# A split of the weight ring, a later clearing of a scratch table, and three changes of order in a two-block transformer kernel

## The chip, the cores and the metric

The kernel runs on one core of a Trainium2 chip. The metric is the device time of one execution in microseconds (us), the median of several runs; lower is better. Engines are named as the profile names them: PE is TensorE, which multiplies matrices (PEld is its weight load), DVE is VectorE, ACT is ScalarE, POOL is GpSimd and SP is SyncE, which issues most of the DMAs.

## What is computed

Two transformer blocks in float32 for one sequence of 256 tokens and a width of 2048. Cut to its stages:

```python
# first block
n1 = rms_norm(x, norm1_gain);  proj = n1 @ w_in          # latents, k_pe, q/k/v of the window heads
o_mla = 8 heads of latent attention (w_q_b, w_kv_b, rope, causal softmax)
o_swa = 16 heads of attention in a window of 128, bias from a table, sinks
h = x + concat(rms_norm(o_mla), rms_norm(o_swa)) @ w_out
q = rms_norm(h) @ peer_w_q;  s = q . sub_keys            # 8 heads, top 16 of 16384 experts for each
y = sum over the chosen experts of  g * gelu(h . expert_u) * expert_v;   h = h + y
# second block
qa, ka, va, qn, kn, vn, gates = rms_norm(h) @ w_in_2
oa = differential attention of 4 heads;   on = neighbourhood attention of 8 heads with a bias
mixed = sigmoid(g_a) * (oa @ w_branch_a) + sigmoid(g_b) * (on @ w_branch_b)
x = h + rms_norm(mixed @ w_out_2)
u = relu(rms_norm(x) @ w_up) ** 2;   out = x + rms_norm(u @ w_down)
```

## The kernel before

All weights stream through one ring. They are cut into 1101 pieces of 128 x 1024 float32 (512 KB), in the fixed order of the list `order`. SP loads a piece into one of five slots of `raw` (L2748). PE multiplies in a reduced float format, so each piece is split in two: ACT writes the rounded high part into one of NH = 3 slots of `whi` (L1872), and DVE then writes the rest, `raw - whi`, into one of three slots of `wlo` (L2102). The activations are split in the same manner: `AA` and `BB` hold 16 blocks of 128 rows with a high half (`AH`, `BH`) and a low half (`AL`, `BL`). A product is then high x high + low x high + high x low. `gemm_piece` keeps the activations as weights in PE and moves the piece past them: 8 matmuls with `whi` and then 4 with `wlo`. `wide_piece` (the stages `peer_w_q`, `peer_u` and `w_up`) keeps the piece in PE and moves the activations past it: 8 matmuls of 512 columns with `whi`, then 8 of 256 columns with `wlo`.

The semaphores of the ring: `hi_split` counts the pieces that ACT split, `lo_split` those that DVE split, and `piece_used` those that PE has finished with. ACT waits for the landing of piece n and for `piece_used` of piece n - 3, DVE waits for `hi_split` of n, SP waits for `lo_split` of n - 5 before it loads n.

The order of work on every engine is written by one function, `walk`. It runs once for each engine; all five runs go through the same steps, and each engine emits only its own instructions. `piece` and `used_up` call `ensure_split`, which puts the loads and splits of the next pieces into the order. Smaller work (transposes, softmax, evacuations) stands in generators in `tasks` and `idle`; `step()` advances each by one `yield` between two pieces. Each engine works strictly in the order that comes out. `fresh(engine, tokens)` leaves out waits that the engine has already passed, and `latest["PE"]` is the last PE mark emitted so far in the walk.

Places that the change and the prediction touch:
- The expert gates are kept in a DRAM table `scr_g` of 16384 x 256 values (16.8 MB). POOL blanks a tile of 128 x 256 (`gate_blank`, L2688) and issues eight DMAs of 2 MB that write zeros from it (`gate_clear`, L2694). Much later POOL adds the chosen gates with 256 indirect DMAs (`gate_scatter`, L2699). In the walk `gate_blank` stands after `queries(1)` of the latent attention; before the change it waits for nothing.
- `k_rope` builds zero-padded rotary keys in two rounds, both in the one slot of `prows`. Each round has a `zero` on POOL (a memset of 128 x 1024, L2680), then `spread_kpe` on DVE (in the trace under L2355), transposes on PE (L1723) and splits. In the order of POOL the first `zero` stands ahead of `gate_blank` and the second one directly behind the eighth `gate_clear`. The scores of the latent attention (`mla_scores`) wait for the splits of both rounds.
- POOL's next instruction after that is `reload_x` (L2685).
- `attend` is the softmax pipeline of all attention units. Behind the exponentials (ACT, L1914) there is one `yield`, then PE turns the probabilities (L1723). `na_unit` uses it for a head of the neighbourhood attention, two units at a time, between the pieces of `w_in_2`.
- `prepare(sc)` multiplies the fetched gelu values by the fetched gates (`expert_gate`, DVE L2507) and splits them into `AA` (ACT L1857, `expert_split` DVE L2514), in four rounds with a `yield` behind each. The first gemm of `peer_v` needs the result of `prepare(0)`. Before, `prepare(0)` is put into `idle` when u is 61, so it runs between the pieces of the units 62 and 63 of `peer_u`. After each unit `u_post` runs: ACT L1857 copies the low sums, DVE L2492 adds, DVE L2498 scales, ACT applies gelu.

Of the kernel before, what the change touches and what calls it, by code (L numbers as in the profile page):

```python
# [37 lines left out]
def build(nc, D, out):  # L38
# [12 lines left out]
    with ExitStack() as ctx:  # L51
# [144 lines left out]
        s_hi, s_lo, s_used = sem("hi_split"), sem("lo_split"), sem("piece_used")  # L196
        s_vec = sem("vector_step")

        def walk(steps):
# [189 lines left out]
            def gemm_wide(name, units, both, toks, post, lead=2):  # L389
                taken = [take(accs) for _ in units]  # L390
                for c in range(4):
                    while len(toks) < min(2 * c + lead, 8):
                        step(0)
                    for n, (u, (pair, free)) in enumerate(zip(units, taken)):
                        i, low = piece(name, 4 * u + c)
                        high = fresh("PE", (s_hi, i + 1))
                        b = [banks[2 * pair], banks[2 * pair + 1]]
                        go("mm_wide", i, b, c, both, high, low, fresh("PE", toks[2 * c:2 * c + 2], free))
                        last = used_up()
                        if c == 3:  # L400
# [105 lines left out]
            def attend(scores, U, nk, scale, sink, pslots, blocks, pv, finish, combine=None, per_head=None, added=None):  # L506
# [30 lines left out]
                yield  # L537
# [388 lines left out]
            go("gate_blank")  # L926
# [422 lines left out]
            def na_unit(h):  # L1349
# [297 lines left out]
        def tensor_program(e):  # L1647
# [7 lines left out]
            def gemm_piece(i, b, c, n, lh, ll, high, low, free, kks=(0, 1)):  # L1655
# [5 lines left out]
                for kk in kks:  # L1661
                    kt = 2 * c + kk
                    w = slice(512 * kk, 512 * kk + 512)
                    for t in range(2):
                        a = slice(128 * t, 128 * t + 128)
                        mm(b[t][:, :], lh[:, kt, a], whi[:, s, w], kt == 0, False)
                        mm(b[t][:, :], ll[:, kt, a], whi[:, s, w], False, False)
# [11 lines left out]
            def gemm_rows(held, t, b, n, lh, ll, free):  # L1679
# [3 lines left out]
                for i, c, split in held:  # L1683
# [3 lines left out]
                    for kk in range(2):  # L1687
# [3 lines left out]
                        mm(b[t][:, :], lh[:, kt, a], wlo[:, s, w], False, False)  # L1691
                        last = mm(b[t][:, :], ll[:, kt, a], whi[:, s, w], False, kt == 2 * n - 1)
                    if t == 1:
                        last.then_inc(s_used, 1)
# [3 lines left out]
            def wide_piece(i, b, c, both, high, low, free):  # L1698
                s = i % NH
                for mark in free:  # L1700
                    e.wait_ge(*mark)
                for mark in high:
                    e.wait_ge(*mark)
                for kk in range(4):
                    kt = 4 * c + kk
                    x = both[:, kt, :, :].rearrange("p a n -> p (a n)")
                    for m in range(2):
                        w = slice(256 * kk + 128 * m, 256 * kk + 128 * m + 128)
                        mm(b[m][:, :], whi[:, s, w], x, kt == 0, False)
                for mark in low:  # L1710
                    e.wait_ge(*mark)
                for kk in range(4):
                    kt = 4 * c + kk
                    for m in range(2):
                        w = slice(256 * kk + 128 * m, 256 * kk + 128 * m + 128)
                        last = mm(b[m][:, 0:256], wlo[:, s, w], both[:, kt, 0, :], False, kt == 15)
                last.then_inc(s_used, 1)
# [15 lines left out]
            def kpe_mm(i, bank, split, free):  # L1733
# [6 lines left out]
                for kt in range(16):  # L1740
                    w = slice(64 * kt, 64 * kt + 64)
                    mm(o, whi[:, s, w], AH[:, kt, :], kt == 0, False)
                    mm(o, wlo[:, s, w], AH[:, kt, :], False, False)
                    last = mm(o, whi[:, s, w], AL[:, kt, :], False, kt == 15)
# [56 lines left out]
            def sub_scores(i, c, q4, t, bank, end, split, ready):  # L1801
# [5 lines left out]
                for m in range(4):  # L1807
# [5 lines left out]
                    mm(o, AH[:, hp, a], wlo[:, s, w], False, False)  # L1813
                    last = mm(o, AL[:, hp, a], whi[:, s, w], False, True)
# [35 lines left out]
            walk({"consts": consts, "mm": gemm_piece, "mm_rows": gemm_rows, "mm_wide": wide_piece, "transpose": transpose, "bias_mm": bias_mm,  # L1850
# [4 lines left out]
        def scalar_program(e):  # L1855
# [205 lines left out]
        def vector_program(e):  # L2061
# [604 lines left out]
        def gpsimd_program(e):  # L2666
# [20 lines left out]
            def gate_blank():  # L2687
                e.memset(blank, 0.0).then_inc(sem("gate_blank"), 1)  # L2688
# [206 lines left out]
```

## Time and profile before

| | us |
|---|---|
| median of 3 runs | 3259.15 |
| range of the runs | 3258.58 to 3262.24 |
| the profiled execution | 3259.14 |
| its span, first to last instruction | 3257.3 |
| PE busy in it | 3200.2 (98%) |
| DVE busy | 2106.2 (65%) |
| ACT busy | 1517.7 (47%) |
| mean granted clock of TensorE | 0.994 |

The profile is of one execution. Its time is the span and 1.8 us around it. A row of the timeline gives the start in us from the span's start, the duration in us, engine, line, operation, out<-in, shapes and how many instructions were merged, and in square brackets how long the engine was idle before it and what released it. "POOL", "DVE" and so on are the engines; an SPq row is the issue of a DMA. The profile's clock is the share of full speed that TensorE was granted: 1.00 is 2.4 GHz and 0.50 is 1.2 GHz.

### The profile page before, as it was taken

The numbers are of one execution on the slowest core, as the hardware profiler recorded it, in microseconds if no ns is written. First come the engines' busy times: TensorE is split into PE (matmuls) and PEld (weight loads), VectorE is DVE, ScalarE is ACT, GpSimd is POOL, SyncE is SP. The second block draws the span as 40 slices with busy tenths as digits, with TensorE's granted clock in tenths as the row PEclk, the third lists the DMA queues.
The fourth block names the chain that finished last, engine by engine and source line by source line (L and its number), as shares of the span: only waits on it lengthen the run. The fifth ranks groups of instructions, "written<-read, shape, count | busy, mean of one in ns | idle before, by whom it ended". The sixth has DMA issues, their size and how long they took to land.

```text
span 3257.3 us, 40800 instructions
## 1 busy us (share of the span) xinstructions
PE 3200.2 (98%) x16112; PEld 2715.7 (83%) x16112; DVE 2106.2 (65%) x3062; ACT 1517.7 (47%) x2006; POOL 492.0 (15%) x322
## 2 busy tenths in 40 slices
PE   8989999999999999999999999999999999999998
PEld 7788888888888888888888888888888788888886
DVE  6766578887555576666666565565465655655556
ACT  5645454545444444444444544445444544444443
POOL 1000005777777200000000000000000000000000
PEclk9999999999999999999999999999999999999999
DMA  8623557888888866666665555444555455555554
GB/s 321 252 85 130 181 183 208 214 214 215 212 214 211 262 249 244 250 248 245 245 233 200 197 184 174 165 170 176 191 194 188 174 192 191 193 189 193 189 192 149
DMA packets 220286, 660.95 MB, mean 203 GB/s; under 512 B 56704, under 2 KB 56848, under 8 KB 217536
## 3 DMA queue, kind: packets, MB, share of 16 engines
q1 hardware_dynamic: 170864, 600.81, 52.9%
q0 software_dynamic: 49232, 57.54, 8.7%
q8 instruction: 127, 2.08, 0.3%
q14 instruction: 63, 0.52, 0.0%
HBM read 622.48 MB, written 35.78 MB: 202 GB/s over the span
## 4 chain that ended last, share of the span: by engine, by line
PE 90%; DVE 6%; ACT 2%; issue 1%; DMA 1%; DVEq 0%; ACTq 0%; SPq 0%
PE PS L1649 89%; DVE wlo L2102 2%; PE PS L1723 2%; ACT whi L1872 1%; DMA raw<-in_w_in_b 0%; DVE R L2606 0%; ACT M L1914 0%; DVE AA L2148 0%; ACT Y L1958 0%; DVE TMP L2177 0%; DVE M L2507 0%; DVE TMP L2178 0%; DVE BB L2148 0%; DMA R<-in_x 0%; DMA M<-in_na_bias 0%
## 5 line engine op out<-in xcount | busy, mean ns | idle before, releaser
L2102 DVE TENSOR_TENSOR wlo<-raw,whi 128x1024 fp32r<-128x1024 f32 x1101 | 1343.8, 1224 | 889.6 <-ACT whi L1872 878.4
L1872 ACT ACTIVATE whi<-raw 128x1024 fp32r<-128x1024 f32 x1101 | 1157.8, 1057 | 1033.4 <-PE PS L1649 998.3
L1649 PE MATMUL PS<-whi,AA 128*128 128x512 f32 (+1 forms) x2880 | 718.7, 390 | 2.0 <-DVE AA L2148 1.2
L1649 PE MATMUL PS<-whi,BB 128*128 128x512 f32 x2640 | 667.4, 393 | 1.7 <-DVE wlo L2102 1.2
L1649 PEld LDWEIGHTS PS<-whi,AA 128*128 128x128 f32 x2880 | 537.0, 189 | 112.4 <-DVE AA L2148 2.0
L1649 PE MATMUL PS<-BB,whi 128*128 128x512 f32 x2304 | 577.4, 392 | 1.7 <-DVE BB L2148 1.7
L1649 PEld LDWEIGHTS PS<-whi,BB 128*128 128x128 f32 x2640 | 491.1, 188 | 102.3 <-DVE wlo L2102 1.8
L2699 POOL DMA_INDIRECT scr_g<-M x256 | 446.9, 1746 | 426.4 <-issue 390.2
L1649 PEld LDWEIGHTS PS<-BB,whi 128*128 128x128 f32 x2304 | 414.4, 189 | 76.1 <-DVE BB L2148 1.9
L1649 PE MATMUL PS<-wlo,AA 128*128 128x512 f32 (+1 forms) x1440 | 389.4, 388 | 1.9 <-DVE wlo L2102 1.9
L1649 PE MATMUL PS<-wlo,BB 128*128 128x512 f32 x1320 | 356.3, 389 | 0.5 <-DVE wlo L2102 0.5
L1649 PEld LDWEIGHTS PS<-BB,wlo 128*128 128x128 f32 x2304 | 314.3, 190 | 22.5
L1649 PE MATMUL PS<-BB,wlo 128*128 128x256 f32 x2304 | 321.2, 282 | 0.0
L1649 PEld LDWEIGHTS PS<-wlo,AA 128*128 128x128 f32 x1440 | 271.2, 188 | 58.0 <-DVE wlo L2102 2.3
L1649 PEld LDWEIGHTS PS<-wlo,BB 128*128 128x128 f32 x1320 | 247.7, 188 | 53.1 <-DVE wlo L2102 0.9
L1649 PE MATMUL PS<-AA,whi 128*128 128x512 f32 (+1 forms) x1056 | 263.8, 391 | 2.6 <-DVE AA L2148 2.2
L1649 PEld LDWEIGHTS PS<-AA,whi 128*128 128x128 f32 (+1 forms) x1056 | 189.4, 188 | 37.2 <-DVE AA L2148 2.8
L1649 PEld LDWEIGHTS PS<-AA,wlo 128*128 128x128 f32 (+1 forms) x1040 | 141.8, 189 | 10.0
L1649 PE MATMUL PS<-AA,wlo 128*128 128x256 f32 (+1 forms) x1040 | 147.2, 282 | 0.0
L1857 ACT ACTIVATE AA<-M 128x512 fp32r<-128x512 f32 x72 | 45.5, 632 | 150.8 <-DVE M L2507 143.8
L1857 ACT ACTIVATE M<-TMP 128x512 f32<-128x512 f32 x64 | 40.5, 633 | 128.1 <-DVE TMP L2498 100.5
L2708 POOL DMA_DIRECT2D M<-scr_a x16 | 8.8, 547 | 589.8 <-DVE AA L2514 543.6
(236 smaller groups left out, 1570.0 us busy)
## 6 DMA issues: line engine op xcount, KB each, us to landing
raw<-in_peer_u SPq DMA_DIRECT2D x256, 512.0 KB
raw<-in_peer_v SPq DMA_DIRECT2D x256, 512.0 KB
raw<-in_w_in SPq DMA_DIRECT2D x160, 512.0 KB
raw<-in_w_up SPq DMA_DIRECT2D x128, 512.0 KB
raw<-in_w_down SPq DMA_DIRECT2D x128, 512.0 KB
raw<-in_w_out SPq DMA_DIRECT2D x64, 512.0 KB
raw<-in_w_in_a SPq DMA_DIRECT2D x32, 512.0 KB
scr_g<-M POOLq DMA_DIRECT2D x8, 2048.0 KB, 30.1
```

The source lines that it names most:

```text
L1649: return e.matmul(outp, l, r, start=start, stop=stop)
L1723: last = e.transpose(banks[bank][:, 128 * n:128 * n + 128], s, ident)
L1857: e.activation(o, x, func, **kw).then_inc(sem(name), 1)
L1872: e.activation(whi[:, n % NH, :], raw[:, n % NR, :], ACT.Copy).then_inc(s_hi, 1)
L2102: e.tensor_tensor(wlo[:, n % NH, :], raw[:, n % NR, :], bf(whi[:, n % NH, :]), ALU.subtract).then_inc(s_lo, 1)
L2699: e.indirect_dma_start(out=D["scr_g"].rearrange("e (t o) -> (e t) o", o=1), out_offset=bass.IndirectOffsetOnAxis(ap=EID[t][:, k:k + 1], ax ...
L2708: e.dma_start(glt[i], D["scr_a"][sc, :, :]).then_inc(sem(f"gelu_fetched{i}"), 16)
```

## The change

There are five edits.

1. `gate_blank` waits for `latest["PE"]`, the last PE mark that was emitted before it: the transpose that also frees the slot `prows` (count 24 of the mark `transposed`). The eight `gate_clear` still wait for `gate_blank` alone.
2. The ring of high parts gets a semaphore of its own, `piece_hi_used`, which PE raises behind the last matmul that reads `whi` of a piece. ACT's split of n now waits for `lo_split` and `piece_hi_used` of n - 3, DVE's split for `hi_split` of n and `piece_used` of n - 3. Where high and low matmuls alternated (`gemm_rows`, `kpe_mm`, `sub_scores`), the one with `wlo` is now last of three.
3. `w_up` with one unit at a time runs its pieces in pairs: 16 matmuls with the two high parts, then 16 with the two low parts, then two calls of `step()`.
4. `attend` takes `slack`, and neighbourhood units pass 1: one more `yield` before the probabilities are turned.
5. `prepare(0)` is put into `idle` when u is 63, behind the last unit of `peer_u`.

```diff
-        s_hi, s_lo, s_used = sem("hi_split"), sem("lo_split"), sem("piece_used")
+        s_hi, s_lo = sem("hi_split"), sem("lo_split")
+        s_hi_used, s_used = sem("piece_hi_used"), sem("piece_used")
...
-                for c in range(4):
-                    while len(toks) < min(2 * c + lead, 8):
+                at_once = 2 if len(units) == 1 and name in ('w_up',) else 1
+                for c0 in range(0, 4, at_once):
+                    while len(toks) < min(2 * (c0 + at_once - 1) + lead, 8):
                         step(0)
...
+                        go("mm_wide", held, [banks[2 * pair], banks[2 * pair + 1]], both)
+                        for _ in held[1:]:
+                            last = up("PE", "piece_used")
+                            step()
                         last = used_up()
...
-                yield
+                for _ in range(1 + slack):
+                    yield
                 bank, bfree = yield from wait_for(misc)
                 tk = transposed([ps[:, 128 * n:128 * n + 128] for n in range(blocks)], bank, te, bfree)
...
-            go("gate_blank")
+            go("gate_blank", fresh("POOL", latest["PE"]))
             t_blank = up("POOL", "gate_blank")
...
-                if u == 61:
+                if u == 63:
                     idle.append(prepare(0))
...
-                                             masked))
+                                             masked), slack=1)
...
             def split(n):
                 e.wait_ge(s_raw[n % NR], 16 * (n // NR + 1))
                 if n >= NH:
-                    e.wait_ge(s_used, n - NH + 1)
+                    e.wait_ge(s_lo, n - NH + 1)
+                    e.wait_ge(s_hi_used, n - NH + 1)
                 e.activation(whi[:, n % NH, :], raw[:, n % NR, :], ACT.Copy).then_inc(s_hi, 1)
...
             def split(n):
                 e.wait_ge(s_hi, n + 1)
+                if n >= NH:
+                    e.wait_ge(s_used, n - NH + 1)
...
-            def gate_blank():
+            def gate_blank(ready):
+                for mark in ready:
+                    e.wait_ge(*mark)
                 e.memset(blank, 0.0).then_inc(sem("gate_blank"), 1)
```

## Rows read from the trace of the kernel before

**Rows 1.** The page: busy us, share of the span and instructions of each engine.
```profile
PE 3200.2 (98%) x16112; PEld 2715.7 (83%) x16112; DVE 2106.2 (65%) x3062; ACT 1517.7 (47%) x2006; POOL 492.0 (15%) x322
```

**Rows 2.** Waits of PE, whole span: who waited for whom, us, times, longest.
```profile
PE PS L1723 <- ACT M L1914: 8.6, 7, 2.9
...
PE PS L1649 <- DVE wlo L2102: 4.3, 5, 1.9
```

**Rows 3.** Timeline of POOL, 0 to 520 us.
```profile
39.33 0.31 POOL L2688 MEMSET M<- 128x256 f32 x1
39.93 8.00 POOL L2694 DMA_DIRECT2D scr_g<-M  x7 [0.30 <-POOL M L2688]
105.00 1.12 POOL L2694 DMA_DIRECT2D scr_g<-M  x1 [57.07 <-issue]
154.68 0.95 POOL L2680 MEMSET M<- 128x1024 f32 x1 [48.56 <-PE PS L1723]
```

**Rows 4.** DMA, POOL's queue, 39 to 104 us: packets, MB, share of 16 engines.
```profile
q0 software_dynamic: 3695, 14.68, 58.8%
```

**Rows 5.** The same queue, 44 to 54 us, when it has the DMA engines alone.
```profile
DMA packets 912, 3.67 MB, mean 367 GB/s; under 512 B 17, under 2 KB 17, under 8 KB 912
q0 software_dynamic: 911, 3.67, 102.2%
```

**Rows 6.** The same, 109 to 111 us and then 52 to 54 us.
```profile
q0 software_dynamic: 197, 0.81, 102.7%
...
q0 software_dynamic: 160, 0.66, 103.5%
```

**Rows 7.** SP's DMA queue, 155.3 to 163 us.
```profile
q1 hardware_dynamic: 180, 0.61, 25.1%
```

**Rows 8.** Timeline, 146 to 168 us: the path around the second zero.
```profile
156.21 0.75 DVE L2355 TENSOR_TENSOR M<-M,ST 128x256 f32<-128x256 f32 x2
...
157.02 5.78 PE L1723 MATMUL PS<-C,M 128*128 128x128 f32 x28 [2.40 <-DVE M L2355]
...
167.00 1.01 PE L1649 MATMUL PS<-BB,AA 128*128 128x256 f32 x3 [4.20 <-DVE AA L2148]
```

**Rows 9.** Timeline of DVE, 38 to 52 us.
```profile
43.42 3.77 DVE L2281 TENSOR_SCALAR TMP<-TMP 128x64 f32<-128x64 f32 x1
...
48.26 0.20 DVE L2294 TENSOR_SCALAR TMP<-TMP 128x64 f32<-128x64 f32 x1
```

**Rows 10.** Timeline, 1128 to 1152 us: a unit's end, then one round of the first preparation.
```profile
1135.61 2.00 PE L1649 MATMUL PS<-BB,whi 128*128 128x512 f32 x8
...
1136.44 0.69 DVE L2492 TENSOR_TENSOR TMP<-TMP,PS 128x512 f32<-128x512 f32 x1 [1.04 <-ACT TMP L1857]
...
1138.53 0.76 DVE L2507 TENSOR_TENSOR M<-M 128x256 f32<-128x256 f32 x2
1139.32 0.63 ACT L1857 ACTIVATE AA<-M 128x512 fp32r<-128x512 f32 x1 [1.96 <-DVE M L2507]
1139.99 0.69 DVE L2514 TENSOR_TENSOR AA<-M,AA 128x512 fp32r<-128x512 f32 x1 [0.70 <-ACT AA L1857]
```

**Rows 11.** The page's groups: a split of a piece on ACT; busy us, mean ns, idle before.
```profile
L1872 ACT ACTIVATE whi<-raw 128x1024 fp32r<-128x1024 f32 x1101 | 1157.8, 1057 | 1033.4 <-PE PS L1649 998.3
```

**Rows 12.** Busy time by stretch, engines in order, then clock, DMA share, GB/s.
```profile
230.00:240.00 10.00, 8.27 (x38) 7.37 (x39) 7.14 (x32) 5.50 (x21) 0.00 (x0) 0.66 0.22 85
1060.00:1200.00 140.00, 139.85 (x747) 120.45 (x747) 87.58 (x100) 66.81 (x78) 25.06 (x21) 1.00 0.78 268
2600.00:3230.00 630.00, 630.00 (x3171) 537.05 (x3170) 369.17 (x371) 275.21 (x296) 0.00 (x0) 1.00 0.55 190
```

**Rows 13.** Waits of PE, 2160 to 2230 us.
```profile
PE PS L1723 <- ACT M L1914: 2.0, 3, 0.8
```

**Rows 14.** Timeline of PE, 2552 to 2560 us: one piece of w_up.
```profile
2554.82 2.00 PE L1649 MATMUL PS<-AA,whi 128*128 128x512 f32 x8
2556.66 1.11 PE L1649 MATMUL PS<-AA,wlo 128*128 128x256 f32 x8
```

More of the change, by code:

```diff
@@ L390, in gemm_wide @@
                 taken = [take(accs) for _ in units]
-                for c in range(4):
-                    while len(toks) < min(2 * c + lead, 8):
+                at_once = 2 if len(units) == 1 and name in ('w_up',) else 1
+                for c0 in range(0, 4, at_once):
+                    while len(toks) < min(2 * (c0 + at_once - 1) + lead, 8):
                         step(0)
                     for n, (u, (pair, free)) in enumerate(zip(units, taken)):
[L395 to L398, printed above, removed]
+                        held = []
+                        for c in range(c0, c0 + at_once):
+                            i, low = piece(name, 4 * u + c, NH - 1 - (c - c0))
+                            held.append((i, c, fresh("PE", (s_hi, i + 1)), low, fresh("PE", toks[2 * c:2 * c + 2], free)))
+                        go("mm_wide", held, [banks[2 * pair], banks[2 * pair + 1]], both)
+                        for _ in held[1:]:
+                            last = up("PE", "piece_used")
+                            step()
                         last = used_up()
-                        if c == 3:
+                        if held[-1][1] == 3:
                             post(u, pair, last)
@@ L504, in walk, with attend @@
             alt = [0]
-            def attend(scores, U, nk, scale, sink, pslots, blocks, pv, finish, combine=None, per_head=None, added=None):
+            def attend(scores, U, nk, scale, sink, pslots, blocks, pv, finish, combine=None, per_head=None, added=None, slack=0):
                 bank, bfree = yield from wait_for(misc)
@@ L1696, in gemm_rows, with wide_pieces @@
                     last.then_inc(sem("rows_done"), 1)
[L1698 to L1717, printed above, removed]
+            def wide_pieces(held, b, both):
+                for i, c, high, low, free in held:
+                    for mark in free:
+                        e.wait_ge(*mark)
+                    for mark in high:
+                        e.wait_ge(*mark)
+                    for kk in range(4):
+                        kt = 4 * c + kk
+                        x = both[:, kt, :, :].rearrange("p a n -> p (a n)")
+                        for m in range(2):
+                            w = slice(256 * kk + 128 * m, 256 * kk + 128 * m + 128)
+                            last = mm(b[m][:, :], whi[:, i % NH, w], x, kt == 0, False)
+                    last.then_inc(s_hi_used, 1)
+                for i, c, high, low, free in held:
+                    for mark in low:
+                        e.wait_ge(*mark)
+                    for kk in range(4):
+                        kt = 4 * c + kk
+                        for m in range(2):
+                            w = slice(256 * kk + 128 * m, 256 * kk + 128 * m + 128)
+                            last = mm(b[m][:, 0:256], wlo[:, i % NH, w], both[:, kt, 0, :], False, kt == 15)
+                    last.then_inc(s_used, 1)
             def transpose(srcs, bank, ready):
@@ L1742, in kpe_mm @@
                     mm(o, whi[:, s, w], AH[:, kt, :], kt == 0, False)
-                    mm(o, wlo[:, s, w], AH[:, kt, :], False, False)
-                    last = mm(o, whi[:, s, w], AL[:, kt, :], False, kt == 15)
+                    high = mm(o, whi[:, s, w], AL[:, kt, :], False, False)
+                    last = mm(o, wlo[:, s, w], AH[:, kt, :], False, kt == 15)
+                high.then_inc(s_hi_used, 1)
                 last.then_inc(s_used, 1)
@@ L1812, in sub_scores @@
                     mm(o, AH[:, hp, a], whi[:, s, w], True, False)
-                    mm(o, AH[:, hp, a], wlo[:, s, w], False, False)
-                    last = mm(o, AL[:, hp, a], whi[:, s, w], False, True)
+                    high = mm(o, AL[:, hp, a], whi[:, s, w], False, False)
+                    last = mm(o, AH[:, hp, a], wlo[:, s, w], False, True)
+                if end:
+                    high.then_inc(s_hi_used, 1)
                 last.then_inc(s_used if end else sem("sub_scores"), 1)
```

12 lines of the change are left out of this document (8 added, 4 removed).

## The prediction, made before the changed kernel was run

> **What bounds the kernel now.** I read the page first: PE is busy for 3200.2 us of a span of 3257.3 us [rows 1], so all that PE can gain by better order is 57 us, while any new wait of PE goes into the time one for one. Next the waits of PE: they are short and few [rows 2]. Then the stretches: from 2600 to 3230 us PE is busy for 630.00 of 630.00 us, and from 1060 to 1200 us for 139.85 of 140.00 [rows 12]. So the changed semaphores of the ring, the pairs in w_up and the later preparation act where PE has nothing to win. The idle time lies in the first 350 us, around the two attentions and at the ends. The rest I read off the timelines of POOL and of the path to the first attention scores [rows 3, 8], and off the DMA queues [rows 4 to 7].
>
> **Part 1, the clearing: what it removes.** Before, POOL issues seven clears from 39.93 us on [rows 3], and the DVE instructions beside them are slow: one of 128 x 64 takes 3.77 us where its like takes 0.20 a little later [rows 9]. DVE is in order, so the low part behind it comes late, and the longest wait of PE for a low part, 1.9 us at about 50 us [rows 2], follows. Without the clears there I take it as gone: -1.9 us. The weight loads that share the DMA engines with the clears are late too, but PE waits for them for some tenths only: -0.3 us. Bounds of both together: 0 to -3.
>
> **Part 1: what it puts in the way.** The second `zero`, which starts at 154.68 [rows 3], stands in POOL's order directly behind the eighth clear. It is on the path: it ends at 155.63, DVE spreads the keys into its tile at 156.21, PE turns them from 157.02 on, and the first scores start at 167.00 after PE was idle for 4.20 us, waiting for DVE [rows 8]. DVE has at most 0.6 us of slack there. Before, POOL came to the `zero` long before it was needed and sat idle for 48.56 us [rows 3]. Now `gate_blank` waits for the same transpose that the `zero` waits for, so blank and eight issues come between.
> How long do eight issues take? The key is in the POOL timeline: seven go out in 8.00 us, the eighth only at 105.00, after 57.07 us in which POOL waited for nothing that the trace names [rows 3]. By 104 us POOL's queue had moved 14.68 MB [rows 4], which is seven times 2.097 MB: the eighth clear was issued 1 us after the bytes of all seven were through. So POOL can't issue an eighth DMA of this size until the seven ahead are drained, and whatever stands behind it waits too. The changed kernel comes to this point with the same DMAs in POOL's queue, in the same order, and all earlier ones landed.
> The new times, step by step. Blank starts at 154.7, the first clear 0.6 us later, as before (39.33 to 39.93), at 155.3. First bytes move some 3 us after (an estimate: first issue at 39.93 [rows 3], and from 44 us on the queue is at full rate [rows 5]): 158.3. The queue alone moves 367 GB/s [rows 5], so 14.68 MB take 40.0 us; SP's loads beside it are 0.61 MB [rows 7], 1.7 us more. Drained at 200.0, eighth issue at 201.0, with its 1.12 us [rows 3] and a gap of 0.3 us the `zero` starts at 202.4 less the overlap, say 202.1, and ends at 203.1. DVE's spread starts at 203.2 in place of 156.2: +47.0 us. Of the 10.8 us from spread to scores [rows 8] about 1 us is waiting for work of PE and ACT that is by then done: +46.0 us.
> Bounds: at the higher rate of 0.81 MB in 2 us and without the startup and the loads beside it 14.68 MB take 36.2 us, and the term is +37; at 0.66 MB in 2 us [rows 6] they take 44.5 us, and it is +51. I take 46 because the 10 us of rows 5 are the longest stretch in which this queue is alone. PE loses its clock in such a pause, but it does so in this place already.
> The Trainium skill (SBUF — State Buffer, section SBUF: two separate sides) gives about 358 GB/s between HBM and one core. That page's figure would make 14.68 MB an estimated 41.0 us instead of 40.0 and the sum 1 us longer; the trace's 367 GB/s is close to it.
> Behind the `zero` on POOL stands only `reload_x`, which waits for the end of this attention anyhow.
>
> **Part 2, the ring.** Nothing is added on PE but a semaphore increment; ACT may split a piece one low part earlier, DVE at the same time as before or earlier, since it no longer has ACT's copy between the freed slot and its own work. No engine waits longer for what it waited for before. In all, PE waits 4.3 us for low parts [rows 2], and 1.9 of these are counted above; part of the 8.6 us for exponentials [rows 2] hangs on DVE being held up by a split. Bounds 0 to -4, taken -1.5 us. The changed order of three matmuls keeps their number and shapes: 0.
>
> **Part 3, the pairs.** One piece of w_up takes 1.84 us with the high part (2554.82 to 2556.66) and 0.95 with the low part [rows 14]. A pair has the same matmuls. PE never waits from 2600 to 3230 us [rows 12], and with three slots the low part that comes latest in a pair is needed over 3 us after its slot is free. 0, bounds -1 to +2. If that cover is gone, each of some 60 pairs could wait for a split of about 1 us [rows 11].
>
> **Part 4, the slack.** PE waits three times, 2.0 us in all, for the exponentials of the neighbourhood heads [rows 13]. One more piece between exponentials and turn covers the longest of them, 0.8 us. The units get four steps longer in all, so the last turns leave the shadow of the pieces and come back to back; they wait for nothing. -2.0 us, bounds 0 to -2.
>
> **Part 5, the later preparation.** Before, the first preparation begins at 1138.53 [rows 10] and has the whole of two units for its four rounds. Now it begins when PE is through with the last unit, and the first piece of peer_v needs round one. On the path: from the end of the unit's matmuls to the end of DVE's sum 1.52 us (1135.61 to 1136.44 + 0.69), then one round of gate, high part and low part, 1138.53 to 1140.68, 2.15 us [rows 10]: PE waits 3.7 us. The split of the third piece stands behind all four rounds and the scaling: 1.5 + 4 x 2.15 + 0.7 = 10.8, less overlap 10.0, plus ACT's copy of 1.06 [rows 11], so at 11.0 us. PE is ready for it after its wait and two pieces of 12 matmuls, 3.7 + 2 x 2.76 = 9.2 us (12 x 1.84 / 8 [rows 14]): 1.8 us more. Together +5.5 us. What it gives back is at most the 0.15 us that PE is idle in that stretch [rows 12]. Between 230 and 240 us the granted clock was 0.66 after a wait of 2.9 us [rows 2, 12], which costs up to 3.4 us; here I add 1.5. Term +7.0 us, bounds +3.6 to +9.
>
> **Sum.** -2.2 + 46.0 - 1.5 + 0 - 2.0 + 7.0 = +47.3 us. The profiled execution took 3259.14 us, 0.01 us from the median of the three runs, so: 3306.4 us.
>
> **The rivals.**
> - *The eighth clear isn't held.* For it: the trace names no cause for the 57 us. Against it: the byte count fits seven clears to the packet. Then only the issues stand in the way: 8 x 1.14 = 9.1 us from 155.3, the `zero` ends at 165.4, the spread starts 9.3 us later. 9.3 - 2.2 - 1.5 - 2.0 + 7.0 = +10.6: 3269.8 us.
> - *Faster.* The `zero` is not what the path waits for, because the remaining turns and splits of the queries fill the time until the keys are there, and the eighth issue isn't held; and the rounds of preparation find their place under the matmuls. Its gains are at their upper bounds: -3 - 4 - 2 = -9: 3250.2 us. It decides when the spread starts by 156.8 us. Against it are DVE's order, in which the splits stand behind the spread, and PE's idle 4.20 us.
> - *Nothing seen.* The clearing costs nothing and the gains of 5.7 us are eaten by part 5's 5.5: within 2 us of 3259.
>
> **How the numbers follow.** Forecast 0.87, first rival 0.06, faster 0.04, nothing seen 0.03. Low end: 37 - 3 - 4 - 2 - 1 + 3.6 = +31; high end: 51 + 2 + 9 = +62. Not all terms end on one side at once, so the range is 3293 to 3319; the cases outside it hold less than 2 in 10. About 0.2% (6.5 us) is what a measurement can tell from no change here. Slower by more than that: forecast and first rival, 0.93; faster 0.04; same 0.03.
>
> **What would show it.** In the POOL timeline: blank at 154 us or a little earlier, seven clears, then a gap of 36 to 45 us ahead of the eighth, and the `zero` right behind it; POOL's DMA queue full in between. In PE's waits: one of some 40 us for DVE L2355 or L1723 near 160 us, the first scores near 213. In DVE, L2281 down from 3.77 to 0.2 us and no wait of PE at 50 us. At the end of peer_u a wait of 3 to 4 us for DVE L2514, and one of 1 to 2 us for ACT L1872 two pieces later. No wait for L1914 in w_in_2. The prediction is wrong if the eighth clear goes out within 10 us of the seventh.

## The result, and the profile after

The changed kernel took 3305.63 us (median of 4 runs, 3304.98 to 3305.75), beside 3258.86 us for the kernel before on the same chip: a ratio of 1.0143, interval 1.0127 to 1.0159. It is 47 us slower, 0.8 us from the forecast. The line numbers have moved: the matmul is L1656 (was L1649), the turn L1735 (L1723), the low split L2120 (L2102), the high split L1888 (the L1872 of rows 11), the spread of the keys L2373 (L2355), the clear L2714 (L2694), the `zero` L2698 (L2680), the scatter L2719 (L2699).

The page of after: busy us, share and instructions of each engine, to be held against rows 1.
```profile
PE 3195.2 (97%) x16112; PEld 2714.1 (82%) x16112; DVE 2093.6 (63%) x3062; ACT 1520.6 (46%) x2006; POOL 520.2 (16%) x322
```
PE does the same 16112 matmuls in a span that is 45.9 us longer, and is not busier for it: the time is idleness of PE, at one place, as its waits show (who waited for whom, us in total, times, longest):
```profile
PE PS L1735 <- DVE M L2373: 52.5, 2, 52.1
...
PE PS L1656 <- DVE AA L2532: 3.5, 1, 3.5
...
PE PS L1656 <- DVE wlo L2120: 2.1, 3, 1.2
PE PS L1656 <- ACT whi L1888: 1.8, 4, 0.6
```
The first row is the pause. Rows 2 had 4.3 us of waits for `wlo`; here are 2.1. The second row is new and belongs to part 5. POOL's timeline holds the cause of the pause, to be read against rows 3:
```profile
151.41 0.31 POOL L2708 MEMSET M<- 128x256 f32 x1 [112.99 <-PE PS L1735]
152.01 8.00 POOL L2714 DMA_DIRECT2D scr_g<-M  x7 [0.30 <-POOL M L2708]
200.51 1.12 POOL L2714 DMA_DIRECT2D scr_g<-M  x1 [40.50 <-issue]
201.55 1.04 POOL L2698 MEMSET M<- 128x1024 f32 x1
```
Seven issues, 40.50 us in which POOL stands and the trace names no event, the eighth, the `zero`. The path from there, in the timeline of all engines, against rows 8:
```profile
202.63 0.76 DVE L2373 TENSOR_TENSOR M<-M,ST 128x256 f32<-128x256 f32 x2 [50.06 <-POOL M L2698]
...
203.44 5.33 PE L1735 MATMUL PS<-C,M 128*128 128x128 f32 x28 [52.10 <-DVE M L2373]
...
213.43 1.01 PE L1656 MATMUL PS<-BB,AA 128*128 128x256 f32 x3 [4.66 <-DVE AA L2166]
```
The first scores start at 213.43 in place of 167.00. The trace also has the landing of every clear: the first lands at 161.3 us, the seventh at 200.0, and the eighth is issued at 200.51. In before these three are 49.9, 104.5 and 105.00. So the hold ends with the landing of the last clear ahead. Between POOL's first clear and the eighth the DMA engines do this (152 to 200 us; first the rate in 40 slices of it, then the sum, POOL's queue q0 and SP's q1):
```profile
GB/s 355 198 352 294 331 321 331 341 321 331 335 328 331 335 317 335 335 321 324 341 328 324 341 317 331 331 331 328 328 335 324 341 328 341 341 348 314 215 215 79
DMA packets 3829, 15.14 MB, mean 315 GB/s; under 512 B 133, under 2 KB 133, under 8 KB 3829
...
q0 software_dynamic: 3696, 14.68, 92.3%
q1 hardware_dynamic: 133, 0.46, 2.4%
```

Where the time went can be followed along the whole span. The n-th matmul of PE is the same one in both kernels up to small exchanges inside a piece or a pair, so the start of one in after less its start in before gives how late the kernel is at that point. I took these from the two traces:

```
point                          before, us   after - before, us
near the start                    14.8          -0.7
past the wait at 50 us            62.7          -3.6
just ahead of the keys           149.1         -3.7
first attention scores           167.0         +46.4
twelve us ahead of peer_v       1146.3         +45.4
start of peer_v                 1158.0         +49.1
sixteen us into peer_v          1174.4         +53.2
before the neighbourhood heads  1909.8         +52.8
behind the neighbourhood heads  2277.7         +49.3
start of w_up                   2562.6         +47.4
late in w_up                    3155.8         +45.8
```

### The profile page after: what moved, and what is told of

Read it like the earlier page. It is cut to its first block, busy times and chain, and to the rows that moved or that the text cites. A ratio compares the mean times of both kernels' runs of the same rounds, so it can differ in the third digit from the quotient of the medians.

```text
span 3303.2 us, 41898 instructions
## 1 busy us (share of the span) xinstructions
PE 3195.2 (97%) x16112; PEld 2714.1 (82%) x16112; DVE 2093.6 (63%) x3062; ACT 1520.6 (46%) x2006; POOL 520.2 (16%) x322
## 4 chain that ended last, share of the span: by engine, by line
PE 91%; DVE 4%; issue 2%; ACT 1%; POOL 0%; DMA 0%; DVEq 0%; ACTq 0%; SPq 0%
PE PS L1656 90%; PE PS L1735 1%; DVE wlo L2120 1%; ACT whi L1888 1%; POOL scr_g L2714 0%; DVE R L2624 0%; ACT M L1930 0%; DVE AA L2166 0%; DVE M L2525 0%; DVE M L2229 0%; DMA R<-in_x 0%; DVE BB L2166 0%; DVE Y L2268 0%; ACT Y L1974 0%; DVE RT L2105 0%
## 5 line engine op out<-in xcount | busy, mean ns | idle before, releaser
L2120 DVE TENSOR_TENSOR wlo<-raw,whi 128x1024 fp32r<-128x1024 f32 x1101 | 1339.8, 1223 | 796.0 <-ACT whi L1888 667.3
L1888 ACT ACTIVATE whi<-raw 128x1024 fp32r<-128x1024 f32 x1101 | 1154.3, 1057 | 823.4 <-PE PS L1656 761.3
L1656 PE MATMUL PS<-whi,AA 128*128 128x512 f32 (+1 forms) x2880 | 718.9, 390 | 7.0 <-DVE AA L2532 3.5
L1656 PE MATMUL PS<-whi,BB 128*128 128x512 f32 x2640 | 666.7, 393 | 1.7 <-DVE wlo L2120 1.2
L1656 PEld LDWEIGHTS PS<-whi,AA 128*128 128x128 f32 x2880 | 536.3, 188 | 118.5 <-DVE AA L2532 4.6
L1656 PE MATMUL PS<-BB,whi 128*128 128x512 f32 x2304 | 577.4, 392 | 1.7 <-DVE BB L2166 1.7
L1656 PEld LDWEIGHTS PS<-whi,BB 128*128 128x128 f32 x2640 | 491.2, 188 | 102.3 <-DVE wlo L2120 1.6
L2719 POOL DMA_INDIRECT scr_g<-M x256 | 475.0, 1855 | 432.1 <-issue 391.0
L1656 PEld LDWEIGHTS PS<-BB,whi 128*128 128x128 f32 x2304 | 414.3, 189 | 76.1 <-DVE BB L2166 1.9
L1656 PE MATMUL PS<-wlo,AA 128*128 128x512 f32 (+1 forms) x1440 | 388.6, 387 | 0.0
L1656 PE MATMUL PS<-wlo,BB 128*128 128x512 f32 x1320 | 356.3, 389 | 0.5 <-DVE wlo L2120 0.5
L1656 PEld LDWEIGHTS PS<-BB,wlo 128*128 128x128 f32 x2304 | 314.3, 190 | 22.5
L1656 PE MATMUL PS<-BB,wlo 128*128 128x256 f32 x2304 | 321.2, 282 | 0.0
L1656 PEld LDWEIGHTS PS<-wlo,AA 128*128 128x128 f32 x1440 | 271.1, 188 | 55.9
L1656 PEld LDWEIGHTS PS<-wlo,BB 128*128 128x128 f32 x1320 | 247.7, 188 | 53.1 <-DVE wlo L2120 1.0
L1656 PE MATMUL PS<-AA,whi 128*128 128x512 f32 (+1 forms) x1056 | 252.1, 389 | 1.8 <-DVE AA L2166 1.8
L1656 PEld LDWEIGHTS PS<-AA,whi 128*128 128x128 f32 (+1 forms) x1056 | 193.3, 188 | 39.2 <-DVE AA L2166 2.2
L1656 PEld LDWEIGHTS PS<-AA,wlo 128*128 128x128 f32 (+1 forms) x1040 | 134.0, 190 | 5.3
L1656 PE MATMUL PS<-AA,wlo 128*128 128x256 f32 (+1 forms) x1040 | 137.9, 282 | 0.0
L1872 ACT ACTIVATE AA<-M 128x512 fp32r<-128x512 f32 x72 | 45.5, 633 | 162.6 <-DVE M L2525 155.7
L1872 ACT ACTIVATE M<-TMP 128x512 f32<-128x512 f32 x64 | 40.5, 633 | 153.3 <-DVE TMP L2516 125.8
L2383 DVE TENSOR_TENSOR R<-R,PS 128x512 f32<-128x512 f32 x128 | 82.1, 683 | 45.5 <-PE PS L1656 45.5
```

Source lines behind the costliest of these rows:

```text
L1656: return e.matmul(outp, l, r, start=start, stop=stop)
L1872: e.activation(o, x, func, **kw).then_inc(sem(name), 1)
L1888: e.activation(whi[:, n % NH, :], raw[:, n % NR, :], ACT.Copy).then_inc(s_hi, 1)
L2383: last = e.tensor_tensor(R[:, t, c], R[:, t, c], b[t][:, :], ALU.add)
L2719: e.indirect_dma_start(out=D["scr_g"].rearrange("e (t o) -> (e t) o", o=1), out_offset=bass.IndirectOffsetOnAxis(ap=EID[t][:, k:k + 1], ax ...
```

## The experiments

Offsets given below are of this kind, against the kernel before, from one profiled execution each.

**Edit 1 alone.** The kernel before with the one wait added.
```diff
-            go("gate_blank")
+            go("gate_blank", fresh("POOL", latest["PE"]))
```


> The kernel before with edit 1 alone (gate_blank waits for latest PE). Theory (POOL holds the eighth clear until the seven ahead are through, and the second zero stands behind it): +46 us against before, 1.0141; the eighth clear 40 us after the seventh, the zero right behind it, PE idle for some 50 us ahead of the turns at 203 us. Rival (the pause needs the new ring semaphores or another edit): under 1.003, no pause.

Measured: 3307.88 us, ratio 1.0148 (1.0132 to 1.0163). The offset is +46.9 at the first scores and +49.7 at the end. The whole slowdown is there without the other four edits.

**All but edit 1.** The changed kernel with the clears back in their place.
```diff
-            go("gate_blank", fresh("POOL", latest["PE"]))
+            go("gate_blank", [])
```


> The changed kernel with gate_blank waiting for nothing, as before. Theory: edits 2 to 5 together are worth about +7.6 (preparation) - 3.4 (slack) - 1.3 (ring at the start of w_up) - 1.4 (pairs) = +1.5 us, 1.0005, and the waits of PE at 50 and 62 us are as in the kernel before. Rival (the pause comes from the rest of the change): 1.013 or more. Rival for the first 60 us (the ring, not the moved clears, freed the wait at 50 us): PE doesn't wait for a low part there.

Measured: 3258.2 us, ratio 0.9999 (0.9990 to 1.0008). The four other edits together are worth nothing that can be measured: -0.7 us at the first scores, +5.1 in peer_v, +1.3 behind the neighbourhood attention, -1.0 at the end. At 50 us it is 1.7 us ahead, at 62.7 only 0.6, where edit 1 alone is 2.7 ahead: nearly all of the gain at the front in after is the clearing's, and the ring does not bring it alone.

**The clears behind the second `zero`.** They keep the late place, but the `zero` goes first; `prepare(0)` at u = 61.
```diff
-            go("gate_blank", fresh("POOL", latest["PE"]))
-            t_blank = up("POOL", "gate_blank")
-            for c in range(8):
-                go("gate_clear", c, fresh("POOL", t_blank))
-                t_clear = landing("gate_cleared")
             while len(qt_done) < 6 or len(kt_done) < 8 or not t_rq:
                 step()
+            go("gate_blank", fresh("POOL", latest["PE"]))
+            t_blank = up("POOL", "gate_blank")
+            for c in range(8):
+                go("gate_clear", c, fresh("POOL", t_blank))
+                t_clear = landing("gate_cleared")
```


> The changed kernel with blank and clears put behind the second zero in POOL's order, and the preparation at u = 61 again. Theory: no pause, the gains at 50 and 62 us stay (-3.6), the slack (-3.4), the ring (-1.3) and the pairs (-1.4) too: -9.7 us against before, 0.997, 3249 us. The eighth clear goes out about 40 us after the seventh, near 200 us, with reload_x behind it, which needs to go at 208. Rival (the DMA traffic of the clears itself, 335 GB/s over 45 us, holds up the attention): slower than before by 10 us or more.

Measured: 3267.43 us, ratio 1.0023 (1.0014 to 1.0032). The pause of PE is gone, and with it 38 us (41 against the next run, which has the pause and the same u = 61), but the kernel doesn't reach what I expected. POOL's timeline in this kernel, and two waits of PE over its whole span:
```profile
151.12 0.95 POOL L2698 MEMSET M<- 128x1024 f32 x1 [112.96 <-PE PS L1735]
158.15 0.31 POOL L2708 MEMSET M<- 128x256 f32 x1 [6.08 <-PE PS L1735]
158.76 7.98 POOL L2714 DMA_DIRECT2D scr_g<-M  x7 [0.30 <-POOL M L2708]
211.22 1.12 POOL L2714 DMA_DIRECT2D scr_g<-M  x1 [44.48 <-issue]
```
```profile
PE PS L1656 <- ACT whi L1888: 8.3, 4, 7.6
...
PE PS L1656 <- DVE Y L2268: 5.0, 1, 5.0
```
The eighth issue is held as ever, 44.48 us, but behind it stands only `reload_x`, which is not due yet. The scores start 3.8 us earlier than in before; at 218 us the kernel is 3.9 us late. The loss of 7.7 us begins with the second row of the waits, 5.0 us. It falls in the latent attention, where the bias table of the window heads is built beside the scores. The timelines of DVE and of PE:
```profile
203.22 1.28 DVE L2268 SCALAR_TENSOR_TENSOR Y<-POS,C,R 128x1024 f32<-128x1024 int32 x1 [4.56 <-DMA R<-in_key_pos]
```
```profile
204.56 7.09 PE L1656 MATMUL PS<-ST,Y 128*128 128x64 f32 x32 [5.00 <-DVE Y L2268]
```
DVE waits 4.56 us for a load of key positions, on which before had no wait at all; here it runs while the clears fill the DMA engines. PE then takes 7.09 us for 32 matmuls at half the clock (0.50 from 201.1 to 214.8 us), where the 32 ahead of the pause took 3.68: 3.4 us more. With the 5.0 us, less the 0.7 us that PE waits at this place in before, that makes the 7.7. The other row, 7.6 us at a stretch, ends at 1156.78 us, in the last units of peer_u, 16 us ahead of the start of peer_v, and was not in my reckoning at all. The next two runs go after it.

**Edit 5 undone.** The changed kernel, `prepare(0)` as before.
```diff
-                if u == 63:
+                if u == 61:
```


> The changed kernel with the first preparation at u = 61 as before. Theory: the wait of 3.5 us for the first gated block and three of 0.5 us for a split go, and the half clock behind them: -7.6 us against the changed kernel, 3298 us, +39 us against before, 1.012. Rival (the waits move elsewhere): 3304 to 3306 us, 1.014.

Measured: 3308.35 us, ratio 1.0150 (1.0137 to 1.0164), so 2.7 us above the changed kernel where I had expected to be some 7 below it. The intervals of the two ratios overlap; that it is not 7 us faster is sure, and the traces show the loss at this place: from 1060 to 1174.4 us the offset rises by 10.6 us here and by 7.7 in the changed kernel. Waits of PE over the whole span, then of DVE from 1100 to 1230 us:
```profile
PE PS L1656 <- ACT whi L1888: 8.1, 4, 7.4
```
```profile
DVE M L2525 <- DMA M<-scr_g: 10.5, 1, 10.5
```
DVE stands 10.5 us for the gated values that POOL fetches from memory. In before these were fetched at 1089.9 us, 49 us ahead of their use at 1138.53 [rows 10]; here at 1183.9. With DVE stand the splits that are queued behind the preparation, and so PE. The fetch is behind 256 scatters on POOL, and these take longer:
```profile
L2719 POOL DMA_INDIRECT scr_g<-M x256 | 482.1, 1883 | 437.9 <-issue 394.0 <-DMA scr_g<-M 43.9
```
In before this row has 1746 ns, and in edit 1 alone 1748: it is one of the other edits.

**The ring alone.** The kernel before with edit 2; nothing else of the change.
```diff
             def split(n):
                 e.wait_ge(s_raw[n % NR], 16 * (n // NR + 1))
                 if n >= NH:
-                    e.wait_ge(s_used, n - NH + 1)
+                    e.wait_ge(s_lo, n - NH + 1)
+                    e.wait_ge(s_hi_used, n - NH + 1)
...
             def split(n):
                 e.wait_ge(s_hi, n + 1)
+                if n >= NH:
+                    e.wait_ge(s_used, n - NH + 1)
```


> The changed kernel with edits 1, 3, 4 and 5 undone, so the kernel before with the ring's semaphores and the order of the matmuls in gemm_rows, kpe_mm and sub_scores. Theory A (the ring moves DVE's work under the scatters of POOL and makes them slower): the 256 scatters take 1.85 us and more on average instead of 1.75, the first fetch goes out after 1130 us instead of 1090, the first preparation waits some 7 to 10 us for it and the time is +5 to +8 us, 1.002. Theory B (the delay of the fetch comes from the moved clears or another edit): scatters 1.75 us, fetch at 1090, -1 to -2 us, 0.9995.

Measured: 3263.77 us (11 runs, 3253.25 to 3265.94), ratio 1.0012 (1.0003 to 1.0021). The scatters on POOL, and DVE's wait from 1100 to 1230 us:
```profile
L2719 POOL DMA_INDIRECT scr_g<-M x256 | 481.3, 1880 | 436.9 <-issue 394.0 <-DMA scr_g<-M 42.9
```
```profile
DVE M L2525 <- DMA M<-scr_g: 9.4, 1, 9.4
```
The offset is -1.2 us until 570 us, +7.4 at 1146 and +6.8 at the end. So edit 2 by itself makes each scatter 0.134 us longer on the mean, 34 us in all; POOL's idle times between them grow by 11 us. The fetch comes at 1134.2 in place of 1089.9, its data are there only at 1146.8, and peer_v starts late.

What makes a scatter long can be read from the timelines, here two places of this run and then of before:
```profile
1040.56 1.22 DVE L2120 TENSOR_TENSOR wlo<-raw,whi 128x1024 fp32r<-128x1024 f32 x1 [1.65 <-ACT whi L1888]
1040.64 2.57 POOL L2719 DMA_INDIRECT scr_g<-M  x1 [0.30 <-issue]
```
```profile
1044.01 1.56 POOL L2699 DMA_INDIRECT scr_g<-M  x1 [0.30 <-issue]
1044.78 1.23 DVE L2102 TENSOR_TENSOR wlo<-raw,whi 128x1024 fp32r<-128x1024 f32 x1 [0.89 <-ACT whi L1872]
```
A scatter that starts while DVE is in a low split ends 1.42 us after that split, however long the split still had to go; one that starts ahead of a split takes 1.55 us, and the split that begins during it changes nothing. I counted this over all 256 in both traces. In before 100 start inside a split and take 1977 ns on the mean, the other 156 take 1598; with the ring it is 129 with 2132 ns, and 127 with 1624 (the few long ones among these start inside another operation of DVE). The end 1.42 us behind the split holds to 0.06 us for 98 of the 100 and 128 of the 129. The ring shifts the splits in time so that more scatters run into one, and earlier in it.

Two of the 11 runs took 3253 to 3255 us, some 10 us less than the rest, and a third one 3259.46; one of the 11 runs with the clears behind the `zero` is 8 us and more below its others (3258.75). The step has the size of the loss at the fetch, but no trace of such a run was taken, and whether the fetch comes in time in them is not known.

**Edit 5 alone.** The kernel before with `prepare(0)` at 63; its fetch comes in time (1088.9 us, scatters 1732 ns).
```diff
-                if u == 61:
+                if u == 63:
```


> The kernel before with edit 5 alone. My step in the prediction (PE waits for round one, 3.7 us, and for the third piece's split, 1.8 us, and loses some clock): +7.0 us, 1.0021, range +5 to +9. Rival (the rounds find room): within 1 us of before.

Measured: 3266.47 us, ratio 1.0025 (1.0016 to 1.0034), the offset +7.7 us across the start of peer_v and +7.6 at the end. Waits of PE, 1100 to 1230 us:
```profile
PE PS L1649 <- DVE AA L2514: 3.5, 1, 3.5
PE PS L1649 <- ACT whi L1872: 1.6, 3, 0.6
```

**Only the eighth clear behind the `zero`.** The changed kernel; seven issues stay ahead of it.
```diff
-            for c in range(8):
+            for c in range(7):
...
             while len(qt_done) < 6 or len(kt_done) < 8 or not t_rq:
                 step()
+            go("gate_clear", 7, [])
+            t_clear = landing("gate_cleared")
```


> The changed kernel, only the eighth clear put behind the second zero on POOL. Theory (POOL holds an eighth DMA of 2 MB until the seven ahead are through; what stands behind seven isn't held): the zero starts at about 160 us, right behind seven issues of 8.0 us, and the scores at about 172 in place of 213; some 8 us come back behind it, since the traffic of the clears now meets the window attention: 3268 to 3276 us. Rival (the seven issues themselves block POOL until their bytes are through): the zero stays at 200 us and the time at 3305.

Measured: 3271.99 us, ratio 1.0041 (1.0026 to 1.0056). POOL's timeline:
```profile
151.59 7.98 POOL L2716 DMA_DIRECT2D scr_g<-M  x7 [0.30 <-POOL M L2710]
158.83 1.70 POOL L2700 MEMSET M<- 128x1024 f32 x1
202.00 1.12 POOL L2716 DMA_DIRECT2D scr_g<-M  x1 [41.47 <-issue]
```
The `zero` starts right behind seven issues, and the scores are 4.4 us late, not 46. Seven issues pass; it is the eighth that stops POOL. Behind the scores 6.0 us more are lost by 218 us, with a wait of DVE for the key positions as above (3.7 us) and of PE behind it (4.1 us). This is the rival of the prediction in which the eighth isn't held (3269.8 us), made by hand; it comes near that time in part by luck, since the rival had no cost of the clears' traffic.

**Sixteen clears of half the size.** Number or amount?
```diff
-            for c in range(8):
+            for c in range(16):
...
-                rows = D["scr_g"].rearrange("(c p r) t -> c p r t", c=8, p=128)
-                e.dma_start(rows[c], blank.unsqueeze(1).to_broadcast([128, 16, 256])).then_inc(sem("gate_cleared"), 16)
+                rows = D["scr_g"].rearrange("(c p r) t -> c p r t", c=16, p=128)
+                e.dma_start(rows[c], blank.unsqueeze(1).to_broadcast([128, 8, 256])).then_inc(sem("gate_cleared"), 16)
```


> The changed kernel with sixteen clears of 1 MB instead of eight of 2 MB. If POOL holds by bytes or descriptors, 14 or 15 go out at once and the next one is held for about 40 us; if it holds by the number of DMAs, 7 go out, and the others follow in steps or after about 20 us. In both cases the zero comes at about 200 us, 3300 to 3310 us. The program is otherwise the same.

Measured: 3308.06 us (one run). POOL's timeline:
```profile
151.49 13.09 POOL L2714 DMA_DIRECT2D scr_g<-M  x15 [0.30 <-POOL M L2708]
203.53 0.85 POOL L2714 DMA_DIRECT2D scr_g<-M  x1 [38.95 <-issue]
204.31 1.04 POOL L2698 MEMSET M<- 128x1024 f32 x1
```
Fifteen of 1.05 MB go out without a stop (15.7 MB), the sixteenth is held for 38.95 us. So it is not a count of DMAs. Held is the DMA that would make 16.8 MB in the queue: the eighth of 2.1 MB as well as the sixteenth of 1.05. It goes out 0.6 us after the fifteenth has landed. Bytes and packets halve together here, so the run doesn't tell which of them is counted.

**The clears where nobody waits.** The changed kernel, with blank and clears moved behind the window attention, ahead of the second half of `w_out`; `prepare(0)` at u = 62, between two units.
```diff
             while idle:
                 step()
             everything = everyone()
+            go("gate_blank", fresh("POOL", latest["PE"]))
+            t_blank = up("POOL", "gate_blank")
+            for c in range(8):
+                go("gate_clear", c, fresh("POOL", t_blank))
+                t_clear = landing("gate_cleared")
             r_os, t_os = row_factor(OS, list(os_done.values()))
...
-                if u == 63:
+                if u == 62:
```


> The changed kernel with blank and clears put behind the window attention, ahead of the second half of w_out (about 290 us), and the first preparation at u = 62. Theory: no pause in the latent attention, no traffic of the clears beside the two attentions, the clears are through by about 400 us, ahead of the scatters at 515. Gains of 3.7 (start) + 3.4 (slack) + 1.3 (ring) + 1.4 (pairs) us, less 0 to 4 us for a preparation whose fetch lands at about 1150 us: 3249 to 3254 us, 0.998. Rival (POOL's issues and the traffic slow down DVE and the loads wherever they stand): at or above the kernel before.

Measured: 3250.75 us, ratio 0.9977 (0.9967 to 0.9986): faster than both kernels. POOL's timeline in it:
```profile
288.53 8.00 POOL L2714 DMA_DIRECT2D scr_g<-M  x7 [0.30 <-POOL M L2708]
354.72 1.12 POOL L2714 DMA_DIRECT2D scr_g<-M  x1 [58.19 <-issue]
510.03 1.84 POOL L2719 DMA_INDIRECT scr_g<-M  x1 [154.19 <-DVE M L2497]
```
The eighth is held for 58.19 us, but POOL's next work is at 510 us. Seven pass here too, although `reload_x` had sent 2.1 MB through the same queue at 208 us: what has landed doesn't count. The offset is -3.8 us at the scores, -5.0 up to 1158, -1.3 at 1174, -8.3 at the end. With u = 62 the start of peer_v costs 3.7 us in place of 7.7, with scatters of 1859 ns still.

**The same place with the old waits of the ring** and u = 61; pairs and slack stay.
```diff
-                    e.wait_ge(s_lo, n - NH + 1)
-                    e.wait_ge(s_hi_used, n - NH + 1)
+                    e.wait_ge(s_used, n - NH + 1)
...
-                if n >= NH:
-                    e.wait_ge(s_used, n - NH + 1)
...
-                if u == 62:
+                if u == 61:
```


> The same place of the clears, with the ring's waits as in the kernel before and the preparation at u = 61; the pairs and the slack stay. Theory A (the ring's waits are what makes the scatters slow): scatters 1.75 us on average, first fetch near 1090 us, no wait in the preparation, -3 (start) - 2.6 (slack) - 1 (pairs): 3252 to 3254 us, 0.998, level with the other. Rival: the scatters are as slow as in the changed kernel, and the preparation waits 7 us: 3260.

Measured: 3252.25 us, ratio 0.9980 (0.9971 to 0.9989), scatters 1743 ns, fetch at 1087.4. The offset is -4.1 us and stays there through the start of peer_v, where nothing is lost; -7.1 at the end. The two versions lie too close together to be told apart. Nearly all that these edits gave in any version is had without the ring: the clears moved to this place, the slack and the pairs.

## Why the prediction was right, step by step

**The hold was the step that decided.** Rows 3 and 4 say that the eighth clear went out 1 us after the bytes of seven were through, and the prediction put the `zero` behind that. After shows it at the same place of the order, and three runs say that it is this and nothing else: edit 1 alone has the pause, taking only the eighth from in front of the `zero` leaves 10.5 us of PE's 52.1 us wait there, and with halved clears it falls on the sixteenth.

**The size of the hold.** Expected were a gap of 36 to 45 us and the scores near 213; measured are 40.50 us and 213.43. Yet the working was off at two points that met. The drain doesn't run at the 367 GB/s of rows 5: from 152 to 200 us it is 315 GB/s on the mean, startup included, and most slices of that window lie between 314 and 341. From first clear to eighth issue are 48.5 us where I had 45.7. And the blank started 3.3 us earlier than I said (151.41, not 154.7): my times were on the scale of before and left out the gain at the front, which came out larger as well. PE's wait was 52.1 us where my list of signs had some 40; by the prediction's own times it should have said 49 (PE free at 154.6, the turns at 204.0), so that was a slip. Seen from where the front left off (-3.7), the obstacle is +50.1 us, not +46.0, near the upper bound that rows 6 gave (+51). That the scores came at 213 all the same is luck. Ten microseconds of a transfer of some sixty were too few to take a rate for the whole of it from. The Trainium skill (SBUF — State Buffer, section SBUF: two separate sides) has about 358 GB/s between HBM and a core, by which the drain would be an estimated 41.0 us; in the window above no stretch of several slices reached it.

**The front.** I had -2.2 us; measured -3.7 at 149.1 us, of which -0.7 is there at 14.8 us already, ahead of the clears, with -0.2 to -1.4 at that point in the other kernels: most likely chance between executions. Edit 1 alone has -2.5 us from 14.8 to 62.7 us, so the clearing's own gain was sized well. No wait of PE for `wlo` is left from 39 to 130 us, where before had 2.2 us of them; edit 1 alone has none either, and with the clears back in their place 1.9 us stay. DVE in after, 38 to 52 us, the operation that took 3.77 us in rows 9:
```profile
40.26 0.20 DVE L2299 TENSOR_SCALAR TMP<-TMP 128x64 f32<-128x64 f32 x1
```

**Part 2, the ring.** I had -1.5 us, bounds 0 to -4, from the sentence "No engine waits longer for what it waited for before". That was the false step, and the one real miss. Alone the ring gives -1.2 us until 570 us, then costs 8.6 (+7.4 at 1146), and gives 1.2 back between 1880 and 2000 us, in small steps that no listed wait accounts for. I had looked at PE, ACT and DVE, and not at POOL, whose scatters run beside DVE's work. In before the first fetch behind them has 49 us of lead over its use; the slower scatters and the idle times between them eat 44 of these, and the fetch itself takes 10 to 12. In the changed kernel edit 5 hides this: it starts the preparation so late that the fetch is there (1171.6 us, the gated values used from 1204.8 on).

**Part 3, pairs.** I had 0, measured -1.5 us through w_up. Timeline of PE in after, one pair, against the two rows of a piece in rows 14:
```profile
2607.43 3.82 PE L1656 MATMUL PS<-AA,whi 128*128 128x512 f32 x16
2611.08 2.08 PE L1656 MATMUL PS<-AA,wlo 128*128 128x256 f32 x16
2613.00 3.36 PE L1656 MATMUL PS<-AA,whi 128*128 128x512 f32 x14
```
A pair takes 5.57 us (2607.43 to 2613.00), two pieces took 5.58 (2 x 2.79). Over the 60 pairs of w_up the offset falls by 1.5 us, 0.025 us a pair. It falls by as much in the other kernels with pairs (from +0.5 to -1.0 with edit 1 taken out, for one), and by 0.0 in the three kernels that have only edit 1, 2 or 5. PE is at work without a gap in both, so what shrinks is inside the matmuls' stream; that it is the number of changes between high and low parts is a guess.

**Part 4, slack.** I had -2.0 us, measured -3.5 us between 1909.8 and 2277.7 (+52.8 to +49.3). No wait of PE is left from 2230 to 2290 us, the place of rows 13 shifted. The mechanism was right, the term somewhat too small. Of the -3.5 us, -0.9 lie ahead of 2151 us, and there the ring alone has them too (+8.0 to +7.1), while the version without the ring's waits has none. From 2151 to 2277.7 it is -2.6 us in every kernel with the slack, with the ring or without, and between -0.6 and +1.2 in the three that lack it: edit 1 alone, the ring alone and edit 5 alone.

**Part 5.** I had +7.0 us (3.7 + 1.8 + 1.5). After shows the wait at the first piece and the lower clock behind it (0.63 from 1207 to 1210 us), in PE's timeline:
```profile
1207.02 3.14 PE L1656 MATMUL PS<-whi,AA 128*128 128x512 f32 x8 [3.47 <-DVE AA L2532]
...
1217.66 2.08 PE L1656 MATMUL PS<-whi,AA 128*128 128x512 f32 x8 [0.56 <-ACT whi L1888]
...
1221.20 2.09 PE L1656 MATMUL PS<-whi,AA 128*128 128x512 f32 x8 [0.54 <-ACT whi L1888]
```
Eight matmuls take 3.14 us in place of 2.00. The waits are 3.5 us for DVE and three longer ones for ACT of up to 0.6 us. Across the start of peer_v, 1146.3 to 1174.4, the offset rises by 7.7 us (+45.4 to +53.2), as it does with edit 5 alone. The size was right. What failed is "What it gives back is at most the 0.15 us", true as read in before, but not in the kernel that it is put into: undoing edit 5 there made the kernel 2.7 us slower (+55.2 at 1146, +49.2 at the end), since with the ring's late fetch u = 61 loses more (10.6 us) than u = 63 does (7.7 us).

**Sum.** Said: -2.2, +46.0, -1.5, 0, -2.0, +7.0. Measured along the span: front -3.7, obstacle +50.1, drift behind the scores -1.0, start of peer_v +7.7, drift -0.4, neighbourhood heads -3.5, from there to the start of w_up -1.9, w_up -1.5: +45.8, which is the end's offset. The ring has its part in the front and in 0.9 of the -3.5; its cost at the fetch doesn't show beside edit 5. The -1.9 is of no edit that I can name. The total is nearer than its terms: +4.1 on the obstacle and +0.7 on part 5 stand against -6.3 us on all the others (-12.0 measured, -5.7 said). So the nearness of the sum, 0.8 us, is luck; that the change costs some 47 us because of the hold is not.

## What to carry to other kernels

A DMA issue isn't free for what stands behind it on its engine: look in the trace of the kernel before for an issue that comes late with no releaser named, add up the bytes ahead of it, and don't put such a run of issues in front of anything on the path. A bulk transfer belongs where its issuing engine has nothing to do for the whole of its length, as in the version at 288 us that beat both kernels. And when an edit shifts the work of one engine, look also at the engines that neither feed it nor wait for it: how far ahead of its use does each of their transfers land, and what slows them?

## What the runs showed of the hardware

- A plain DMA issued by POOL is held when the queue would reach 16.8 MB with it (seven of 2.1 MB or fifteen of 1.05 MB pass). It isn't let go when the first ahead has landed, 39 to 55 us earlier, but when all have: in eleven kernels with clears of 2.1 MB the eighth is issued 0.49 to 0.51 us after the seventh has landed. The holds are 57.07, 40.50, 44.48, 41.47 and 58.19 us in five of them.
- Zeros written from SBUF to memory by this queue went at 314 to 341 GB/s for most of 44 us in after; in before there is a stretch of 10 us with 367.
- 256 indirect scatters on POOL took 1746 ns on the mean in before, and 1855 to 1888 ns in every kernel with the ring's own semaphore, 1732 to 1748 in the ones without. The instructions and their data are the same. A scatter that starts inside a low split of DVE ends 1.42 us after the split; 100 of 256 do so in before, 129 with the ring alone. The split keeps its 1.22 us. In rows 9 it is the other way round: there DVE is slowed beside POOL's issues (3.77 against 0.20 us), while seven issues take 8.00 us with DVE at work or without.
- Clears spread under the scores of the latent attention, with the bias table beside them, cost PE 7.7 us there, and under the second half of `w_out` nothing that the offsets show (-3.8 at the scores, -5.0 up to 1158).
